# Splitting the attention scores' operands: stacked rope cross terms, a single buffer for half the cached pages, and key pieces split behind transposes

## The reference

```python
def mla_attention(q_lat, q_pe, ckv, kpe, past_ckv, past_kpe):
    ...
        s = (jnp.einsum('bqhr,bkr->bhqk', ql, kc) + jnp.einsum('bqhd,bkd->bhqk', qp, kp)).astype(F32) * MLA_SCALE
        s = jnp.where(mask, s, -jnp.inf)
        ...   # samples: also scores against 2048 cached positions, page_table -> pages of 128
            p = jax.nn.softmax(s, axis=-1).astype(ckv.dtype)
            o = jnp.einsum('bhqk,bkr->bqhr', p, kc)
```

## Time and profile before

| | |
|---|---|
| median of 3 runs | 3023.67 us (3023.09 to 3023.96) |
| the profiled execution: device time, span | 3025.1 us, 3023.5 us |
| PE busy | 2819.0 us (93% of the span) |
| DVE busy, ACT busy | 1452.7 us, 1330.1 us |
| granted TensorE clock, mean | 0.965 of full speed |

### The profile page before, as it was taken

How to read it: one execution, slowest core, us unless ns; L and a number is a source line. 1 busy time by engine, 2 the same in 40 slices (tenths; PEclk the granted TensorE clock), 3 DMA queues, 4 the chain that set the end, 5 groups by cost and what they waited for, 6 DMA issues and landing times.

```text
span 3023.5 us, 60725 instructions
## 1 busy us (share of the span) xinstructions
PE 2819.0 (93%) x24504; PEld 2362.7 (78%) x24504; DVE 1452.7 (48%) x2885; ACT 1330.1 (44%) x2026; POOL 44.6 (1%) x78
## 2 busy tenths in 40 slices
PE   6999997888889989999999999999989989999997
PEld 3899885777768868799887899888856667789996
DVE  1544327878758773634425444333433434544433
ACT  2444336555535444634335444344423334544443
POOL 0000000000010000000000000000000000000000
PEclk7999998889899899999999999999999998999998
DMA  6223442212212224222343123432365435322221
GB/s 241 82 89 115 168 159 75 83 64 85 78 68 75 91 96 188 92 83 97 132 183 117 70 97 123 163 146 72 134 186 164 145 112 190 124 75 93 102 96 67
DMA packets 58281, 349.35 MB, mean 116 GB/s; under 512 B 7537, under 2 KB 7874, under 8 KB 28578
## 3 DMA queue, kind: packets, MB, share of 16 engines
q1 hardware_dynamic: 52274, 322.85, 29.8%
q0 software_dynamic: 5872, 24.59, 2.3%
HBM read 334.96 MB, written 12.45 MB: 115 GB/s over the span
## 4 chain that ended last, share of the span: by engine, by line
PE 76%; DVE 8%; ACT 7%; issue 3%; DVEq 2%; DMA 2%; ACTq 0%; PEldq 0%; SPq 0%; POOL 0%; PEld 0%
PE PS L941 54%; PE PS L919 3%; PE PS L955 2%; PE PS L868 2%; PE PS L979 1%; PE PS L1438 1%; PE PS L1420 1%; PE PS L1423 1%; PE PS L1399 1%; PE PS L900 1%; DMA weight_ring<-in_mla_pairs 1%; PE PS L963 1%; PE PS L875 1%; DMA weight_ring<-in_ada_w 1%; DVE arena L2747 1%
## 5 line engine op out<-in xcount | busy, mean ns | idle before, releaser
L2161 DVE TENSOR_TENSOR w_rest<-weight_ring,w_hi 128x1024 bf16<-128x1024 f32 (+1 forms) x268 | 320.8, 1197 | 857.2 <-ACT w_hi L1618 857.0
L1618 ACT ACTIVATE w_hi<-weight_ring 128x1024 fp32r<-128x1024 f32 (+1 forms) x284 | 294.7, 1038 | 889.0 <-PE PS L941 886.2
L941 PE MATMUL PS<-hid_hi,w_hi 128*128 128x260 f32 x2432 | 326.9, 286 | 0.0
L941 PEld LDWEIGHTS PS<-hid_hi,w_hi 128*128 128x128 f32 x2432 | 299.2, 188 | 2.3
L941 PE MATMUL PS<-hid_rest,w_bf 128*128 128x260 bf16 x2432 | 298.4, 274 | 0.0
L941 PE MATMUL PS<-hid_bf,w_rest 128*128 128x260 bf16 x2432 | 296.6, 274 | 0.0
L1619 ACT ACTIVATE w_bf<-weight_ring 128x1024 bf16<-128x1024 f32 (+1 forms) x284 | 289.6, 1020 | 0.0
L941 PEld LDWEIGHTS PS<-hid_bf,w_rest 128*128 128x128 bf16 x2432 | 235.6, 97 | 36.5
L941 PEld LDWEIGHTS PS<-hid_rest,w_bf 128*128 128x128 bf16 x2432 | 223.8, 97 | 38.6
L941 PE MATMUL PS<-gu_hi,w_hi 128*128 128x260 f32 x1232 | 168.7, 288 | 0.0
L941 PEld LDWEIGHTS PS<-gu_hi,w_hi 128*128 128x128 f32 x1232 | 152.8, 188 | 14.1 <-issue 11.2
(11 more groups left out here) (490 smaller groups left out, 4502.4 us busy)
## 6 DMA issues: line engine op xcount, KB each, us to landing
weight_ring<-in_ffn_gu SPq DMA_DIRECT2D x88, 1024.0 KB, 4.8
ada_chunks<-in_ada_w SPq DMA_DIRECT2D x40, 1536.0 KB, 6.5
weight_ring<-in_ffn_wd SPq DMA_DIRECT2D x32, 1408.0 KB, 6.1
weight_ring<-in_w_hgrn SPq DMA_DIRECT2D x16, 1024.0 KB, 4.9
weight_ring<-in_ada_w SPq DMA_DIRECT2D x8, 1536.0 KB, 8.2
weight_ring<-in_w_ssm SPq DMA_DIRECT2D x8, 1536.0 KB, 6.6
weight_ring<-in_mla_pairs SPq DMA_DIRECT2D x8, 1536.0 KB, 6.5
weight_ring<-in_w_out_ab SPq DMA_DIRECT2D x8, 1024.0 KB, 7.9
```

The lines of the kernel that those rows point to most:

```text
L941: last = pe.matmul(PS[:, bank + hf, 0:HT], w[:, k * P:(k + 1) * P], x[:, first + k, hf * HT:(hf + 1) * HT], start=start and w is w_hi and ...
L1618: act.activation(hi, src, ACT.Copy).then_inc(w_hi_ready, 1)
L2161: tt(WL_[:, buf, 0:n], W[:, slot, j * DC * P:j * DC * P + n], WH[:, buf, 0:n].bitcast(F32), ALU.subtract).then_inc(w_rest_ready, 1)
```

## The change

- Scores: the nope query of each head and the keys are taken apart into a high part (`QNH`, `KNH`, fp32r), a bf16 copy (`QNB`, `KNB`) and a bf16 rest (`QNL`, `KNL`). Three matmuls for each block take the place of the fp32 one. The rope product becomes a high x high matmul over 64 rows (`QPH`, `KPH`) and one bf16 matmul over 128 rows, in which both cross terms are stacked: `QPS2` holds the bf16 query and its rest, `KPS2` the key's rest and the bf16 key. The five matmuls of a block stand together.
- ACT makes high parts and bf16 copies, DVE the rests, in functions that are new in their steps (`query_parts`, `rope_parts`, `key_rest`, `query_rest`, `rope_rest`); the key piece out of bank 4 is now copied twice by ACT and read once by DVE.
- `combine` is cut into `page_sum`, `combine` and `page_out`, with rests between them.
- The split tiles take the place of page buffers. The pages of quarters 0 and 1 keep two sets; those of quarters 2 and 3 have one set (`LATE_PAGES`), freed by PE in the middle of `page_mix`, which now goes through quarters 2, 3, 0, 1.

```diff
-        PAGES = [[yar.take(PAGE_W) for _ in range(7)] + [war.take(PAGE_W) for _ in range(7)]
-                 + [ar.take(PAGE_W) for _ in range(2)],
-                 [aar.take(PAGE_W) for _ in range(5)] + [car.take(PAGE_W) for _ in range(6)] + [mar.take(PAGE_W)]
-                 + [ar.take(PAGE_W) for _ in range(4)]]
+        EARLY_PAGES = [[war.take(PAGE_W) for _ in range(7)] + [ar.take(PAGE_W)],
+                       [car.take(PAGE_W) for _ in range(6)] + [mar.take(PAGE_W), ar.take(PAGE_W)]]
+        LATE_PAGES = [aar.take(PAGE_W) for _ in range(5)] + [ar.take(PAGE_W) for _ in range(3)]
+
+        def page_at(jj, quarter, q):
+            return (EARLY_PAGES[jj] if quarter < 2 else LATE_PAGES)[2 * q + quarter % 2]
+
+        har = Arena(HH.rearrange("p a b -> p (a b)"))
+        KNH, QNH, QPH, KPH = har.take(2, NP_), har.take(NP_), har.take(NP_), har.take(NP_)
+        yar = Arena(Y.rearrange("p a b -> p (a b)"), har.at)
+        QNB, QNL, KPS2 = (yar.take(NP_ // 2).bitcast(BF16) for _ in range(3))
+        QPS2 = yar.take(NP_).bitcast(BF16).rearrange("p (a b) -> p a b", a=2)
...
                     def pages_of(i, jj):
                         sp.wait_ge(k_free[jj], i + 1)
-                        for pg in range(NPAGE):
-                            page = sp.value_load(TABLE[0:1, bass.ds(i * (2 * NPAGE) + (jj * NPAGE + pg), 1)],
-                                                 min_val=0, max_val=A["pages"].shape[0] - 1)
-                            sp.dma_start(PAGES[jj][pg], A["pages"][page]).then_inc(k_in[jj], 16)
+                        for quarter in range(4):
+                            if quarter == 2:
+                                sp.wait_ge(k_late_free, i * 2 + (jj + 1))
+                            for q in range(QUARTERS):
+                                pg = 4 * q + quarter
+                                page = sp.value_load(TABLE[0:1, bass.ds(i * (2 * NPAGE) + (jj * NPAGE + pg), 1)],
+                                                     min_val=0, max_val=A["pages"].shape[0] - 1)
+                                sp.dma_start(page_at(jj, quarter, q), A["pages"][page])\
+                                  .then_inc(k_in[jj] if quarter < 2 else k_late_in, 16)
...
                     pe.wait_ge(p_kvc, 4 * n + 2 * half + 1)
+                    pe.wait_ge(key_rest_done, 2 * n + half + 1)
...
                 def scores(n, hh):
                     lo = hh * ROPE
                     pe.wait_ge(p_kvc, 4 * n + 2 * hh + 1)
+                    pe.wait_ge(key_rest_done, 2 * n + hh + 1)
+                    pe.wait_ge(query_hi, 3 * n + hh + 2)
+                    pe.wait_ge(query_rest_done, 3 * n + hh + 2)
                     for qb in (3, 2, 1, 0):
                         if qb == 0:
                             pe.wait_ge(p_oc, n * 2 + hh + 2)
-                        pe.matmul(PS[:, qb, 0:(qb + 1) * P], OC[:, 2 * n + hh, qb * P:(qb + 1) * P],
-                                  KN[:, hh, 0:(qb + 1) * P], start=True, stop=False)
-                    for qb in (3, 2, 1, 0):
-                        pe.matmul(PS[:, qb, 0:(qb + 1) * P], QPE[lo:lo + ROPE, n, qb * P:(qb + 1) * P],
-                                  KPE[lo:lo + ROPE, 0:(qb + 1) * P], start=False, stop=True).then_inc(p_sc, 1)
+                        rows, cols = slice(qb * P, (qb + 1) * P), slice(0, (qb + 1) * P)
+                        out = PS[:, qb, cols]
+                        pe.matmul(out, QNH[:, rows], KNH[:, hh, cols], start=True, stop=False)
+                        pe.matmul(out, QPH[lo:lo + ROPE, rows], KPH[lo:lo + ROPE, cols], start=False, stop=False)
+                        pe.matmul(out, QNB[:, rows], KNL[:, hh, cols], start=False, stop=False)
+                        pe.matmul(out, QNL[:, rows], KNB[:, hh, cols], start=False, stop=False)
+                        pe.matmul(out, QPS2[:, hh, rows], KPS2[:, cols], start=False, stop=True).then_inc(p_sc, 1)
...
-                    for j in range(4):
+                    for j in (2, 3, 0, 1):
                         for q in range(QUARTERS):
-                            pe.matmul(PS[q * QR_:(q + 1) * QR_, 7, 0:RC * P], PTD[:, j, q * QR_:(q + 1) * QR_],
-                                      PAGES[jj][4 * q + j][:, 2 * PAGE:4 * PAGE], start=(j == 0),
-                                      stop=(j == 3 and q > 0))
+                            last = pe.matmul(PS[q * QR_:(q + 1) * QR_, 7, 0:RC * P], PTD[:, j, q * QR_:(q + 1) * QR_],
+                                             page_at(jj, j, q)[:, 2 * PAGE:4 * PAGE], start=(j == 2),
+                                             stop=(j == 1 and q > 0))
+                        if j == 3:
+                            last.then_inc(k_late_free, 1)
...
                 def key_piece(i, jj, hh):
                     act.wait_ge(p_kv, i * 8 + (4 * jj + 2 * hh + 1))
-                    act.activation(KN[:, hh, :], PS[:, 4, :], ACT.Copy).then_inc(p_kvc, 1)
+                    act.activation(KNH[:, hh, :], PS[:, 4, :], ACT.Copy)
+                    act.activation(KNB[:, hh, :], PS[:, 4, :], ACT.Copy).then_inc(p_kvc, 1)
+
+                def query_parts(i, head):
+                    q = OC[:, i * 4 + head, 0:NP_]
+                    act.activation(QNB, q, ACT.Copy)
+                    act.activation(QNH, q, ACT.Copy).then_inc(query_hi, 1)
+
+                def rope_parts(i, jj):
+                    q = QPE[:, i * 2 + jj, 0:NP_]
+                    for hh in range(2):
+                        act.activation(QPS2[0:ROPE, hh, :], q[hh * ROPE:(hh + 1) * ROPE, :], ACT.Copy)
+                    act.activation(QPH, q, ACT.Copy).then_inc(query_hi, 1)
...
                 def mixed(i, jj, hh):
                     act.wait_ge(p_o, i * 4 + (jj * 2 + hh + 1))
+                    apart(act)
                     act.activation(OC[:, i * 4 + (jj * 2 + hh), 0:NP_], PS[:, 0, :], ACT.Copy).then_inc(p_oc, 1)
...
                 def step(i, jj, more):
                     n = i * 2 + jj
                     exponentials(i, jj, 0)
+                    query_parts(i, 2 * jj + 1)
                     transposed(i, jj, 0)
...
                     exponentials(i, jj, 1)
                     if more:
                         value_piece(i, jj + 1, 0)
+                        query_parts(i, 2 * jj + 2)
                     transposed(i, jj, 1)
                     if more:
                         key_piece(i, jj + 1, 1)
+                        rope_parts(i, jj + 1)
                     mixed(i, jj, 1)
                     if more:
                         value_piece(i, jj + 1, 1)
 
...
+                act.activation(KPS2[ROPE:P, :], KPE[ROPE:P, 0:NP_], ACT.Copy)
+                act.activation(KPH, KPE[:, 0:NP_], ACT.Copy).then_inc(rope_key_hi, 1)
+                query_parts(0, 0)
+                rope_parts(0, 0)
...
-                def combine(b, jj):
+                def key_rest(i, jj, hh):
+                    dve.wait_ge(p_kvc, i * 8 + (4 * jj + 2 * hh + 1))
+                    tt(KNL[:, hh, :], PS[:, 4, :], KNH[:, hh, :].bitcast(F32), ALU.subtract).then_inc(key_rest_done, 1)
+
+                def query_rest(i, jj, hh):
+                    dve.wait_ge(query_hi, i * 6 + (3 * jj + 2 * hh + 1))
+                    tt(QNL, OC[:, i * 4 + (2 * jj + hh), 0:NP_], QNH.bitcast(F32), ALU.subtract).then_inc(query_rest_done, 1)
+
+                def rope_rest(i, jj):
+                    dve.wait_ge(query_hi, i * 6 + (3 * jj + 2))
+                    for hh in range(2):
+                        own = slice(hh * ROPE, (hh + 1) * ROPE)
+                        last = tt(QPS2[ROPE:P, hh, :], QPE[own, i * 2 + jj, 0:NP_], QPH[own, :].bitcast(F32), ALU.subtract)
+                    last.then_inc(query_rest_done, 1)
+
+                def page_sum(b):
                     dve.wait_ge(b_ex, b + 1)
                     tt(DST[:, 6:7], DST[:, 4:5], DST[:, 5:6], ALU.add)
                     dve.drain()
                     dve.wait_ge(b_w, b + 1)
                     tt(DST[:, 6:7], DST[:, 6:7], DST[:, 9:10], ALU.mult).then_inc(b_sum, 1)
+
+                def combine(b, jj):
...
+
+                def page_out(b):
                     dve.wait_ge(b_oc, b + 1)
                     dve.tensor_copy(OL[:, :, :, b], PS[:, 7, 432:432 + RC * MH].rearrange("p (a b) -> p a b", a=RC))
...
                     softmax(n, 0)
                     own_max(n)
+                    query_rest(i, jj, 1)
                     common_max(n)
+                    if more:
+                        key_rest(i, jj + 1, 0)
                     softmax(n, 1)
+                    page_sum(n)
+                    if more:
+                        query_rest(i, jj + 1, 0)
+                        key_rest(i, jj + 1, 1)
                     combine(n, jj)
                     if more:
+                        rope_rest(i, jj + 1)
+                    page_out(n)
+                    if more:
                         queries(n + 1)
 
                 queries(0)
```

(27 more changed lines are left out.)

## The result

| | before | changed |
|---|---|---|
| median of the runs, us | 3023.67 (3016.52 to 3024.93) | 3001.48 (2988.97 to 3005.64, 5 runs) |
| profiled execution, us (span) | 3025.1 (3023.5) | 3002.59 (3001.0) |
| PE busy | 2819.0 | 2808.9 (94%) |
| mean granted clock | 0.965 | 0.966 |

The ratio is 0.9932 [0.9908, 0.9957]: faster by 22 us where 30 were forecast. One execution of e6 (its first, the profiled one) took 6850.87 us and one of the kernel before, run beside e1 to e4, took 7187.02; they are in the medians, which they shift by 1.6 us, and not in the ratios. The table of stretches shows the step that answers to the earlier trace rows, in both kernels the third of eight, `step(2)`; the columns are the stretch, its length, busy time of PE, PEld, DVE, ACT and POOL, granted clock, DMA share and GB/s.

The account below looks back on a forecast made before the run. In each head DVE's softmax strand, waiting for PE's scores, was taken to bound the step. From 3023.67 us, scores -33.4, seam +0.7 and start +2.5 sum to -30.2, giving 2993.5; forecast 2990 to 2998, wider range 2987 to 3006.

Parts of the forecast that it names:

- My forecast, 2990 to 2998: Whole kernel: the range given for the changed time in us, around 2993.5, with chance 0.61.
- the first row maximum: Sign in each head: DVE starts its first row maximum 1.4 us after the scores' start, before the change 3.50.
- the transposes: Sign in each head: transposes start 7.9 us after the scores' start, a gain of 2.1 us for each head.
- both holes: Sign: PE still idles ahead of the transposes, about 1.8 us in the first head and 0.5 in the second.
- The two fp32r ones I bound by the mixed run of one-pass matmuls: Scores' first block: two fp32r matmuls of 512 columns, each put at 0.226 us, or 0.25 at most.
- 1.08 to 1.15 us: Scores: time for the first block's five matmuls of 512 columns, three bf16 and two fp32r.
- I take 3.0: Scores: PE's time in us for all four blocks of a head, from 2.7 to 3.2, against 4.70 before.
- The seam: From the second head's transposes to the next scores: 7.34 us becomes 7.35 to 7.55; 0.1 taken, seven times, +0.7 us.
- rival 1: Seam longer by ACT and DVE waiting on each other, 0.5 to 1.2 us a step: 2997 to 3002; chance 0.13.
- The start: Ahead of the first step: PE waits for added copies and rests, twice about 1.25 us, +2.5 us.
- rival 2: Granted clock falls behind PE's holes; one fall in each step gives 3002 to 3011 us; chance 0.12.
- Pages: Late eight pages in a single set: landed 13.0 us after release, costing nothing, with 2.5 us of cover.

Follow-up runs that it names:

- e6: Changed kernel with three edits: rope high product over 128 rows by padded queries, rope parts made by head, dummy matmuls at the start; 2993.31 us, ratio 0.99.
- e1: Kernel before with only the order changed: nope and rope products of a block together, still fp32, no splits; 3016.31 us, ratio 0.9979.
- e4: Changed kernel with the late pages released later, behind the second head's mixed products; 3019.02 us, measured once.
- e2: Changed kernel with the rope's high product over 128 rows, the other head's half of the keys being zero; 2998.58 us, measured once.
- e3: Changed kernel with rope parts made by head, the first behind its own key part, the second in the seam; 2998.7 us, measured once.
- e5: Changed kernel with two dummy matmuls of 8 blocks each between the first step's key piece and value piece; 3000.36 us, measured once.
- e8: Same three edits to the changed kernel as e6, run again for a profile; one execution, 3004.66 us.
- e10: Same three edits to the changed kernel as e6, on another chip, the one used for e9; 2997.98 us, ratio 0.9924.
- e9: Version with three edits (e6) plus six dummy matmuls between page scores and the first head's transposes in each step; 2986.62 us, ratio 0.9892.

## Why the prediction was right in kind and 8 us short

**The mechanism** held: DVE's softmax strand waited for scores, and sooner scores shortened the step. The point was 2993.5, the measurement 3001.48: inside the wide range to 3006, but outside "My forecast, 2990 to 2998", which had 0.61. Of its own signs the first row maximum (1.4 us, measured 1.7), the transposes (7.9, 8.2 and 8.4) and both holes (1.8 and 0.5, measured 0.9 and none) failed, and PE once waited 0.56 us for the rope rests, beyond the 0.5 that was to show it wrong. That the clock held behind such holes "in the seven steps before" is true of six; the first step's hole was 0.90 us.

The Trainium skill's rate for such a stream (TensorE: Matmul & The Clock Gate, "Back-to-back issue gap"), 131 ns at 512 columns, would stand between L1443, L1444 and L1445; the trace has 0.22 us there, as the forecast took it.

**The step that failed** is "The two fp32r ones I bound by the mixed run of one-pass matmuls", and from it "1.08 to 1.15 us" for the first block and "I take 3.0" for all four. That run is all of 128 rows; the scores switch between 128 and 64 inside a block. Measured 1.53 us for the block, and 4.11. The first head gained 1.8 us and not 2.1, the second, where "Both stay holes" fell, 1.6: 2.7 and 4.6 us in eight steps. In the second head PE's late scores took over from DVE, which by its own strand would have been ready at about 1.72 + 6.47 = 8.19 us, an estimate, and not at 8.39. e2 shows the cause by repairing it: with equal rows the four blocks take 3.02 us and the heads 7.9. The late bf16 load behind fp32r is still there in e2, and no part of this loss.

**The seam**, "I take 0.1 us", was 0.4: 2.8 us, not 0.7. Each duration was right, and ACT's rope passes, forecast to end at 5.8 to 6.1, ended at 5.94. But the sum had the rests follow `combine` at once and the scores follow the rests at once: it left out 0.42 us ahead of the rests and 0.14 behind them. Most of that (0.30, from e3's row) is DVE's own time between two operations and not a wait for ACT. This was rival 1 in small, and e3 shows that the strand through the rests was the one that counted.

**The start**, "+2.5", was +2.6 in waits, and +2.4 in all at the full clock (16.0 us in e5 for 13.6): right. The clock, rival 2, came at a place not named, in the start, with 2.7 us (e5). In the steps it fell nowhere, and the last step's fall went, worth 1.1 us. Yet e2, e8 and e10 show how near it was: with the forecast's full gain the hole in front of the first head's transposes is 1.7 (forecast 1.8) and the clock falls in two or three steps. With the changed kernel's hole of 0.9 it fell in no step of four profiles (the changed kernel's two, e3, e5), and with the hole filled in e9 it didn't either; so the missed gain is probably what protected it. The length of the hole alone doesn't decide, since the kernel before had 2.2 us and no fall in six steps.

**Pages**: no cost, right; cover 1.1 to 3.1 us for 2.5 (e4).

**The sum**: 2.7 + 4.6 + 2.1 + 2.5 - 1.1 = 10.8 us short in the stage, which gave -19.3 for -30.2. That the medians differ by 22 and not 19 is unchanged code, as the profiles differ there by 3.2 us; what causes that stays open, and that it helped is luck. The code ahead of the stage alone differs by up to 13 us between these profiles (first key piece at 2198.07 in e9, at 2211.03 in e8), and without the 3.2 us the total would have missed by 11 us and not 8.

## What to carry to other kernels

Before costing a short product by its columns, look at PEld in a stretch with the same sequence of row counts: here each change between 128 and 64 rows kept the next load from being pulled ahead, an fp32r load then added its 0.19 us, and padding 64 rows with zeros to 128 was free. That a load begins late in PEld's rows is not yet a cost: look whether the next matmul starts later for it. When one strand is made faster, work out the other strand's length as closely, since it sets what is left of the gain. Ask of each hole that a change makes or leaves whether the clock stays up behind it; six dummy matmuls in it were worth 5.1 us here, as much as a repair.

## What was not expected of the hardware

- The same eight fp32 products take 4.70 us grouped by row count and 5.88 alternating (e1). Two fp32r matmuls of 512 columns start 0.43 us apart across a change of rows and 0.33 with equal rows (e2).
- A load of fp32r weights takes 0.19 us, of bf16 0.10 (PEld's rows). The first adds to the time where it isn't pulled ahead; the second, late behind fp32r, adds 0.01 to 0.03.
- The clock fell behind holes of 1.7 to 1.9 us in some steps, and held behind one of 2.2 in the same execution (e8). What tells them apart is open.
